# A hybrid decoder step on one core: the order of work in the up projection of the ConvGLU

## The reference, cut to what matters

```python
D_MODEL, D_FF, CONV_W = 1024, 2816, 3
def conv_glu(h, conv_buf, w_up, conv_w, conv_b, w_down):
    up = h @ w_up                          # (T, 2 * D_FF): gate half, value half
    g, u = up[..., :D_FF], up[..., D_FF:]
    gp = jnp.concatenate([conv_buf, g], axis=1)
    gc = conv_b
    for j in range(CONV_W):
        gc = gc + conv_w[j] * gp[:, j:j + T]
    return (jax.nn.gelu(gc, approximate=False) * u) @ w_down, gp[:, T:]
```

## Time and profile before

| | |
|---|---|
| three runs, median (lowest to highest) | 1234.72 us (1234.12 to 1235.18) |
| the profiled execution's own time | 1234.72 us |
| its span, first to last instruction | 1232.9 us |
| busy: PE, DVE, ACT, POOL | 97%, 70%, 49%, 12% |
| mean granted clock of TensorE | 0.997 |
| up projections, steps 1 to 9 | from 299.0 to 507.5 us and from 875.4 to 1084.4 us |

### The profile page before, as it was taken

The page is one execution under the profiler, slowest core; times in us unless marked ns, Lnnn a source line. Parts: engine busy times, 40 slices in busy tenths (PEclk is TensorE's granted clock), DMA queues, the critical chain, the costliest instruction groups (busy, mean ns, idle before and its releaser), DMA issues.

```text
span 1232.9 us, 24153 instructions
## 1 busy us (share of the span) xinstructions
PE 1194.1 (97%) x9630; PEld 896.7 (73%) x9630; DVE 862.7 (70%) x1299; ACT 608.9 (49%) x1027; POOL 147.3 (12%) x285
## 2 busy tenths in 40 slices
PE   7999999999999999999999999999999999999998
PEld 6855777777777777777774456677777777777886
DVE  5744567586887887777763479757777877767664
ACT  6323445456545555454443459847545545544432
POOL 1000010001221121000003200000321211100001
PEclk9999999999999999999998999999999999999999
DMA  8643243235555555436547220022655455445563
GB/s 214 236 104 84 74 134 100 89 96 161 138 123 132 119 121 134 134 105 155 147 110 220 81 70 2 2 70 87 179 129 135 112 128 133 106 118 141 142 180 76
DMA packets 197194, 148.60 MB, mean 121 GB/s; under 512 B 5857, under 2 KB 178779, under 8 KB 196530
## 3 DMA queue, kind: packets, MB, share of 16 engines
q1 hardware_dynamic: 181562, 101.80, 28.6%
q0 software_dynamic: 15552, 45.68, 16.5%
HBM read 109.15 MB, written 9.86 MB: 97 GB/s over the span
## 4 chain that ended last, share of the span: by engine, by line
PE 54%; DVE 21%; DMA 9%; issue 8%; ACT 7%; DVEq 1%; ACTq 0%; SPq 0%; POOL 0%; POOLq 0%
PE PS L823 17%; PE PS L601 15%; PE PS L617 10%; DMA stage<-stage 8%; DVE wL L341 4%; DVE acc L1067 2%; PE PS L757 2%; ACT wH L335 2%; DVE G L1055 1%; ACT hidH L461 1%; DVE ntmp L1086 1%; DVE three L1096 1%; DVE hidL L466 1%; PE PS L1624 1%; PE PS L1644 1%
## 5 line engine op out<-in xcount | busy, mean ns | idle before, releaser
L823 PE MATMUL PS<-hidH,blk 128*128 128x288 f16 x1232 | 228.4, 286 | 3.3 <-ACT val L546 1.5
L341 DVE SCALAR_TENSOR_TENSOR wL<-stage,wH 128x1024 f16<-128x1024 f32 x140 | 170.5, 1220 | 73.9 <-ACT wH L335 73.5
L335 ACT ACTIVATE wH<-stage 128x1024 f16<-128x1024 f32 x140 | 146.0, 1045 | 102.1 <-PE PS L617 61.2
L823 PE MATMUL PS<-hidL,blk 128*128 128x288 f16 x616 | 176.2, 286 | 0.0
L601 PE MATMUL PS<-zH,wH 128*128 128x288 f16 x832 | 170.0, 286 | 0.7 <-DVE zL L662 0.7
L601 PE MATMUL PS<-zL,wH 128*128 128x288 f16 x832 | 170.0, 286 | 0.0
L601 PE MATMUL PS<-zH,wL 128*128 128x288 f16 x832 | 170.0, 286 | 0.0
L823 PEld LDWEIGHTS PS<-hidH,blk 128*128 128x128 f16 x1232 | 120.5, 98 | 34.7 <-ACT val L546 2.8
L601 PEld LDWEIGHTS PS<-zH,wH 128*128 128x128 f16 x832 | 81.3, 98 | 22.0 <-DVE zL L662 1.3
L601 PEld LDWEIGHTS PS<-zH,wL 128*128 128x128 f16 x832 | 81.4, 98 | 20.5
L601 PEld LDWEIGHTS PS<-zL,wH 128*128 128x128 f16 x832 | 81.4, 98 | 20.5
(11 more groups left out here) (433 smaller groups left out, 2531.2 us busy)
## 6 DMA issues: line engine op xcount, KB each, us to landing
stage<-in_w_ffn_up SPq DMA_DIRECT2D x88, 512.0 KB, 3.8
quart<-in_w_ffn_down SPq DMA_DIRECT2D x32, 704.0 KB, 5.7
stage<-stage POOLq DMA_DIRECT2D x54, 256.0 KB, 3.9
stage<-in_w_mlstm_in SPq DMA_DIRECT2D x24, 512.0 KB, 5.0
stage<-in_w_swa_qkv SPq DMA_DIRECT2D x12, 512.0 KB, 4.4
quart<-quart POOLq DMA_DIRECT2D x8, 704.0 KB, 5.4
quart<-mixed POOLq DMA_DIRECT2D x8, 704.0 KB, 5.3
C<-in_state_mlstm_C POOLq DMA_DIRECT2D x4, 1024.0 KB, 7.4
```

The source lines that it names most:

```text
L335: nc.scalar.activation(wH[:, slot, :], stage[:, slot, :], ACT.Copy, scale=WSCALE).then_inc(hi_ready, inc)
L341: nc.vector.scalar_tensor_tensor(out=wL[:, slot, :], in0=stage[:, slot, :], scalar=WSCALE, in1=wH[:, slot, :], op0=ALU.mult, op1=ALU.subtr ...
L823: m = nc.tensor.matmul(down_bank(g), blk[:, g % RING, a, 128 * k:128 * (k + 1)], (hidH, hidL)[b][:, k, HIDDEN[j], :], start=(k == 0 and (a ...
```

## The change

It reorders the lists of all five engines in the up projection:

- ACT runs `s34_high` no longer at the head of a step, before `tap(i - 1, 1)` and `keep(i, "p1")`, but in `step_mid`, after `hidden_turned(i - 1)`; `tap(i, 0)` and `keep(i, "u3")` go ahead of `up_high(v0)`; the order of splits is now v0, n2, v1, g0, g1, s34, where it was v0, n2, g0, v1, s34, g1.
- DVE runs `s34_low(i)` after `hidden_lows(i - 1)`, where it stood before `conv(i - 1, 1)`; then `gate(i, 0)`, `up_low(v0)`, `conv(i, 0)`, `value(c22)`, and only then `up_n2`, which stood ahead of `conv(i, 0)`.
- POOL issues `step_s1(1)` after the home copies, not before them; `step_s3(i)` moves to the head of the next round; `pool_s4` of the first pair of the down projection goes ahead of the last two `tails`.
- SP loads g0, g1, v1, v0 where it loaded g0, v1, v0, g1. What each load waits for is the same part as before.
- In steps 0 and 10 ACT copies each value tile (576 columns) from PSUM to `val` (a new function `value`), and `hidden` reads that copy, where it read PSUM. PE's first product of step 1 waits for both copies.

```diff
-        AT = {"v0": 0, "n2": 2, "g0": 3, "v1": 4, "s34": 6, "g1": 8}
-        LOW = {"v0": 2, "n2": 3, "g0": 4, "v1": 6, "s34": 8, "g1": 9}
+        AT = {"v0": 0, "n2": 2, "v1": 3, "g0": 5, "g1": 6, "s34": 7}
+        LOW = {"v0": 2, "n2": 3, "v1": 5, "g0": 6, "g1": 7, "s34": 9}
...
             def step(i):
-                pe.wait_ge(*((ff["h32"], KF * L + 1) if first else (copied, cb)))
+                pe.wait_ge(copied, cb)
                 product_of(v0, 0, x_quarter(0, 1), 0, True)
-                pe.wait_ge(*((ff["h32"], KF * L + 2) if first else (vals, vb)))
+                pe.wait_ge(vals, vb)
...
+            def value(i, s):
+                act.wait_ge(unit_used, up_base(L, i) + 2 * s + 2)
+                if i:
+                    act.wait_ge(ff["h32"], KF * L + 2 * (i - 1) + s + 1)
+                nc.scalar.activation(val[s], tile_ps(2 * s + 1), ACT.Copy).then_inc(ff["copied"], 1)
...
@@ act_ffn
             def step_mid(i):
                 hidden_raw(i - 1)
                 keep(i, "u2")
                 hidden_turned(i - 1)
+                s34_high(act, L, i - 1)
+                tap(i, 0)
+                keep(i, "u3")
             def step_last(i):
                 up_high(act, L, i, "v0")
-                tap(i, 0)
-                keep(i, "u3")
+                gelu(i, 0)
                 n2_high(act, L, i)
-                up_high(act, L, i, "g0")
-                gelu(i, 0)
                 keep(i, "c21")
                 up_high(act, L, i, "v1")
+                up_high(act, L, i, "g0")
-            up_high(act, L, 0, "v0")
             tap(0, 0)
             gelu(0, 0)
+            value(0, 0)
+            up_high(act, L, 0, "v0")
+            n2_high(act, L, 0)
             tap(0, 1)
-            n2_high(act, L, 0)
-            up_high(act, L, 0, "g0")
             gelu(0, 1)
             up_high(act, L, 0, "v1")
+            value(0, 1)
+            up_high(act, L, 0, "g0")
...
             with act.Fori(2, KH - 2) as i:
-                s34_high(act, L, i - 1)
                 tap(i - 1, 1)
...
@@ dve_ffn, step_first
                 hidden_lows(i - 1)
+                s34_low(dve, L, i)
+                gate(i, 0)
             def step_last(i):
-                gate(i, 0)
                 up_low(dve, L, i + 1, "v0")
-                up_n2(dve, L, i + 1)
                 conv(i, 0)
                 value(i, "c22")
+                up_n2(dve, L, i + 1)
                 n2_low(dve, L, i + 1)
-                up_low(dve, L, i + 1, "g0")
                 value(i, "c12")
                 up_low(dve, L, i + 1, "v1")
                 hidden(i, 0)
             gate(0, 0)
+            conv(0, 0)
             up_low(dve, L, 1, "v0")
-            conv(0, 0)
-            gate(0, 1)
             up_n2(dve, L, 1)
-            conv(0, 1)
             hidden(0, 0)
             n2_low(dve, L, 1)
+            gate(0, 1)
+            conv(0, 1)
+            up_low(dve, L, 1, "v1")
             up_low(dve, L, 1, "g0")
...
             with dve.Fori(2, KH - 2) as i:
                 gate(i - 1, 1)
-                s34_low(dve, L, i)
+                up_low(dve, L, i, "g0")
                 conv(i - 1, 1)
...
@@ pool_ffn
             history(0, 1)
-            step_s1(1)
             pool.wait_ge(unit_used, SEG0[f"up{L}"])
             for home, new, ready in ((tH, newTH, turned_x["high"]), (tL, newTL, turned_x["low"])):
                 pool.wait_ge(ready, KQ * (L + 1))
                 pool.dma_start(home[:, :, :, :], new).then_inc(turned_x["home"], 16)
+            step_s1(1)
...
             pool_s1(pool, L, 0)
+            pool_s4(pool, L, 0)
             tails(KH - 1, 0)
             tails(KH - 1, 1)
-            pool_s4(pool, L, 0)
...
@@ SP, ffn
-                    for what in ("g0", "v1", "v0", "g1"):
+                    for what in ("g0", "g1", "v1", "v0"):
```

More of the change, by code:

```diff
@@ L64 @@
 VALS = 3 * len(MIXED)
-UP_COPIES = 4 * len(MIXED)
+UP_COPIES = 4 * len(MIXED) + 4
 COPIES = UP_COPIES + 3 * PAIRS
@@ L540, in keep_block @@
                 if j == 0:
-                    act.wait_ge(ff["h32"], KF * (L + 1) - 2)
+                    act.wait_ge(ff["h32"], KF * (L + 1))
             elif j != 2:
@@ L771, in step @@
             def step(i):
-                n, vb, cb = up_base(L, i), VALS * L + 3 * i, COPIES * L + 4 * i - 4
-                first = isinstance(i, int)
+                n, vb, cb = up_base(L, i), VALS * L + 3 * i, COPIES * L + 4 * i - 2
                 pe.wait_ge(lo_ready, n + LOW["v0"])
-                pe.wait_ge(*((ff["h32"], KF * L + 1) if first else (copied, cb)))
+                pe.wait_ge(copied, cb)
                 product_of(v0, 0, x_quarter(0, 1), 0, True)
-                pe.wait_ge(*((ff["h32"], KF * L + 2) if first else (vals, vb)))
+                pe.wait_ge(vals, vb)
                 product_of(v0, WQ, x_quarter(1, 1), 3, True)
@@ L806, in pe_ffn @@
             pe.wait_ge(turned_x["home"], 32 * (L + 1))
-            step(1)
-            with pe.Fori(2, KH - 1) as i:
+            with pe.Fori(1, KH - 1) as i:
                 step(i)
@@ L813, in pe_ffn @@
                 whole(last, s, 0)
-                pe.wait_ge(copied, COPIES * L + UP_COPIES)
+                pe.wait_ge(copied, COPIES * L + UP_COPIES - 2)
                 pe.wait_ge(vals, VALS * (L + 1) + 3)
@@ L839, in pe_ffn @@
             pe.wait_ge(ff["gate"], 2 + KF * (L + 1) - 1)
-            pe.wait_ge(ff["h32"], KF * (L + 1) - 1)
+            pe.wait_ge(copied, COPIES * L + UP_COPIES - 1)
             pe.wait_ge(mix["low"], KH * L + KH - 1)
@@ L853, in pe_ffn @@
                         pe.wait_ge(ff["gate"], 2 + KF * (L + 1))
-                        pe.wait_ge(ff["h32"], KF * (L + 1))
+                        pe.wait_ge(copied, COPIES * L + UP_COPIES)
                         if L:
@@ L947, in step_mid @@
                 hidden_turned(i - 1)
+                s34_high(act, L, i - 1)
+                tap(i, 0)
+                keep(i, "u3")
             def step_last(i):
                 up_high(act, L, i, "v0")
-                tap(i, 0)
-                keep(i, "u3")
+                gelu(i, 0)
                 n2_high(act, L, i)
-                up_high(act, L, i, "g0")
-                gelu(i, 0)
                 keep(i, "c21")
                 up_high(act, L, i, "v1")
-            up_high(act, L, 0, "v0")
+                up_high(act, L, i, "g0")
             tap(0, 0)
             gelu(0, 0)
+            value(0, 0)
+            up_high(act, L, 0, "v0")
+            n2_high(act, L, 0)
             tap(0, 1)
-            n2_high(act, L, 0)
-            up_high(act, L, 0, "g0")
             gelu(0, 1)
             up_high(act, L, 0, "v1")
-            keep(1, "p1")
-            s34_high(act, L, 0)
-            up_high(act, L, 0, "g1")
+            value(0, 1)
+            up_high(act, L, 0, "g0")
+            step_first(1)
             step_mid(1)
@@ L985, in act_ffn @@
             up_high(act, L, i, "g0")
-            tap(i, 0)
-            keep(i, "u3")
             gelu(i, 0)
+            keep(i, "c21")
             up_high(act, L, i, "v0")
-            keep(i, "c21")
             tap(i, 1)
@@ L999, in act_ffn @@
             gelu(i + 1, 0)
+            value(i + 1, 0)
             block_high(act, L, 1)
@@ L1002, in act_ffn @@
             gelu(i + 1, 1)
+            value(i + 1, 1)
             hidden_raw(i + 1)
@@ L1077, in hidden @@
                 t = KF * L + 2 * i + s
-                whole = isinstance(i, int) and i in (0, KH - 1)
-                if whole:
-                    dve.wait_ge(unit_used, up_base(L, i) + 2 * s + 2)
+                if isinstance(i, int) and i in (0, KH - 1):
+                    dve.wait_ge(ff["copied"], COPIES * L + s + 1 + (UP_COPIES - 2 if i else 0))
                 elif s == 0:
@@ L1083, in hidden @@
                 else:
-                    dve.wait_ge(ff["copied"], COPIES * L + 4 * i)
+                    dve.wait_ge(ff["copied"], COPIES * L + 4 * i + 2)
                 dve.wait_ge(ff["gelu"], t + 1)
-                nc.vector.scalar_tensor_tensor(out=h32[:, s, :], in0=tile_ps(2 * s + 1) if whole else val[s],
-                                               scalar=1.0 / WSCALE, in1=h32[:, s, :],
+                nc.vector.scalar_tensor_tensor(out=h32[:, s, :], in0=val[s], scalar=1.0 / WSCALE, in1=h32[:, s, :],
                                                op0=ALU.mult, op1=ALU.mult).then_inc(ff["h32"], 1)
@@ L1111, in value @@
             def value(i, which):
-                row, a, bank, done, copy = {"c11": (0, HALF, 3, 2, -3), "c22": (1, 0, 2, 6, -1),
+                row, a, bank, done, copy = {"c11": (0, HALF, 3, 2, -1), "c22": (1, 0, 2, 6, 1),
                                             "c12": (0, 0, 2, 8, None)}[which]
@@ L1272, in pool_ffn @@
                 pool.dma_start(home[:, :, :, :], new).then_inc(turned_x["home"], 16)
+            step_s1(1)
             tails(0, 0)
             history(1, 0)
+            step_s4(1)
             tails(0, 1)
```

(3 more changed lines are left out.)

5 lines of the change are left out of this document (1 added, 4 removed).

## The result

The changed kernel takes 1323.61 us (median of 4 runs, 1321.66 to 1324.66), the kernel before beside it 1234.42 (1233.28 to 1235.18): a ratio of 1.0722, 95% interval 1.0703 to 1.074. The forecast was 1286, range 1268 to 1303: the side was right, but the time lies above the range, and the loss was 89 us where 51 were forecast. The profiled execution took 1317.62 us, its span is 1315.8, 82.9 more than before; that difference is taken apart here. The other executions had a mean granted clock of 0.968 to 0.971, the profiled one 0.973.

The account below looks back on a forecast made before the run. PE's matmuls were taken to bound the steps (22.05 of 23.14 us). Terms 24.6 - 0.6 + 12.8 + 0.65 + 5.4 + 8.4 = 51.3 us, on 1234.72, gave 1286 us, range 1268 to 1303.

Parts of the forecast that it names:

- The wait for keep "p1" goes: Before P4 in the steady steps: PE's longer wait, for ACT's copies, is removed; gain 9.4 us over both layers at most.
- P8 waits for c22, behind v0's load and `v0_low`: Steps 2 to 8: the later `s34_low` puts v0's load into the loop that PE waits for; +24.6 us over both layers.
- P8 waits about 2.7 us; the step is 24.9: Steps 2 to 8: the loop between successive `gate(i, 1)` sums to 24.87 us, against 23.14 before; c22 comes late for P8.
- holds such meetings already: v0's load in the steady loop: median 3.8 us, plus 0.15 until ACT starts, taken to include loads that met others.
- Three waits of over 6 us are new: Clock term: one wait before each step 1 and one before the turning, 2.8 us each; +8.4, bounds 0 and 9.
- The crowded load: Rival for steps 2 to 8: v0's load takes 5 us or more, giving 1303 us and up; chance 0.07.
- The hidden load: Rival: v0 is there in time, P8 waits no more, a step takes 22.3 us, total 1250; chance 0.09.
- Start of the layers: Step 1's P1 waits for ACT's copies and s1 behind the home copies: +5.6 us; with a longer step 1, +6.4 a layer.
- I take the second layer alike: The second layer's start was given the first's +6.4 us, making +12.8 for both.
- The two ends: First layer's last hidden split +0.65 us; second layer's turning of the saved state 7.1 us late, 1.7 hidden, so +5.4.
- the 0.65 for the first layer's end: Step 10's copies of v0 and v1 ahead of `hidden` delay the hidden tile's last split, for which PE waits, by 0.65 us.
- the hidden wait: Second layer's end: 1.7 us of the turning's 7.1 us delay covered, as PE waited behind this point anyway.

## Why the prediction was right in its direction and too small

- *The wait for keep "p1" goes*: right. *P8 waits for c22, behind v0's load and `v0_low`*: right, link by link in the table, and shown by putting c22 first.
- *P8 waits about 2.7 us; the step is 24.9*: 2.8 to 3.5 us idle, and 27.3. Two terms are behind it. The load was taken at the median, with the words that it "holds such meetings already". It came to 4.70 in the mean with ACT's start, where the sum had 3.95, because POOL's s1 is issued 1 us ahead of it; without that it is 3.82. That is 0.75 a step, 10.5 us.
- **The step that failed is the clock's**: "Three waits of over 6 us are new", with 2.8 us for each. The list of new waits long enough to bring the clock down held only the ends, while the text itself had put a new wait into every step, between the 0.9 us that left the clock alone (the 1.50 us in the earlier trace rows did too) and the 3.58 us of the earlier trace rows that did not. It took that one at no cost. Measured are 1.49 us a step in the mean, 21 us in the 14 steps. The three long waits themselves cost 1.3, 1.3 and 2.4 us, 5 together, where the forecast had 8.4. Of the 34 us by which steps 2 to 8 exceed the forecast (58.7 against 24.6) this and the load make 31, gate to conv another 2.
- *The crowded load (1303 and up)* has the measured time, but not its mechanism: it asked for a load of 5 us or more, and even 4.94, the longest of the 14 with ACT's start in it, is under that. That the number falls there is luck.
- *The hidden load (1250)* underrated what remains without the load: the early s34 gives 23.6 us a step, not 22.3, as `v0_high` stands behind tap and keep on ACT.
- *Start of the layers*: right in the first, 5.5 us against 5.6, with its queueing behind the home copies, as putting s1 first shows. "I take the second layer alike" was wrong by 2.9: PE's wait there grew by 8.4. s1 took 10.9 us in place of 8.8, and PE had waited 0.7 us less from start to start before the second layer's P1 than before the first's. The kernels that leave s1 in its place show the second layer's wait at 6.5 to 8.3 us, the first's at 6.1 to 6.4. What makes the second vary is open. Step 1 took 26.05 us, forecast 24.1, the clock's loss and P8's longer wait within it.
- *The two ends*: the turning came 7.5 us later (1190.01 - 1159.06 against 1107.89 - 1084.4), forecast 7.1; step 9 gave 0.5 a layer back, forecast 0.3. Of the 0.65 for the first layer's end 0.2 are seen in PE's wait for the last split (1.2 us against 1.0); other small waits in that down projection add 0.8, whose cause isn't shown.
- *The sum of the profiled execution*: 58.7 (steps 2 to 8) + 5.5 + 8.4 (starts) + 5.0 (both steps 1) - 1.1 (steps 9) + 7.5 (turning) + 1.0 (first layer's down projection) + 0.8 (behind the turning, the clock's loss less the hidden wait) - 2.9 (the fall behind the wait before L617, which the kernel before had and this execution hadn't) = 82.9. The other 6 us of the median, 89 against 83, are in executions with a lower mean clock. The profiles of all ten experiments have the fall before L617's matmuls; that the other executions of the changed kernel had it too, and so about half of the 6 us, is not shown.

The sentence on the Trainium skill's page ("TensorE: Matmul & The Clock Gate", section "HAM oscillation — how this bites in real kernels") describes such a case, a wait in each turn of a loop that lets the clock fall each time. It was applied to the three long waits only; the trace agrees with the page for the loop as well, with 14 falls in the 14 steps.

## What to carry to other kernels

When a walk through the loop gives a new wait of PE, price its clock too: find the longest wait of the trace that left the clock alone and the shortest that did not, and where the new one lies between them, take the fall as possible in every turn, not as absent. One trace of one wait doesn't settle it: the wait before L617 let the clock fall in eleven profiles and left it alone in the twelfth. Where a slot's release moves later in a list, follow the ring of release, load and split back to the release; moving the consumer only lets another product wait (23.6 us a step), moving the release breaks it (22.1). A median load time doesn't cover a transfer that the new order puts beside that load every time.

## What was not expected of the hardware

- Waits of PE of 2.4 to 2.95 us from start to start brought the clock to 0.50 in 8 of 14 steps and left it in 6 (s1 after v0's load), and the length didn't decide which: 2.43 did, and 2.95 did not. At 3.1 to 3.7 us (the changed kernel) it fell in all 14, at 1.6 to 2.0 (the changed kernel with s34 early) in none. But two longer waits left it at 1.00: 3.87 us before L617 in the changed kernel, and 3.89 us before the second layer's step 1 with s1 first.
- Putting 24 unused matmuls into such waits made the kernel 17.5 us faster.
- A DMA of 256 KB within SBUF, issued 1 us ahead of a load of 512 KB, made the load 0.9 us longer in the mean (4.70 against 3.82 from issue to first use).
